# Which engine squares and adds the pairs of x behind the two mixer outputs

## What is computed

```
def rms_norm(x, g):
    y = xf * lax.rsqrt(jnp.mean(xf * xf, axis=-1, keepdims=True) + EPS)
for layer in range(DEPTH):          # DEPTH = 2: recurrent mixer, then attention mixer
    hn = rms_norm(x, norm_mix_g[layer])
    mix = rglru_mixer(hn, ...) if layer % 2 == 0 else dsa_mixer(hn, ...)
    x = x + mix
    x = x + sq_relu_mlp(rms_norm(x, norm_mlp_g[layer]), mlp_w_up[layer], mlp_w_down[layer])
```

## Time and profile before

| | us |
|---|---|
| median of 3 runs | 905.74 |
| lowest, highest | 905.62, 906.69 |
| time of the profiled execution | 907.54 |
| its span in the profile | 905.9 |
| PE busy in it | 874.5 |
| DVE busy | 688.9 |
| ACT busy | 469.6 |
| POOL busy | 161.1 |

### The profile page before, as it was taken

How to read it: one execution, slowest core, us unless ns; L and a number is a source line. 1 busy time by engine, 2 the same in 40 slices (tenths; PEclk the granted TensorE clock), 3 DMA queues, 4 the chain that set the end, 5 groups by cost and what they waited for, 6 DMA issues and landing times.

```text
span 905.9 us, 17923 instructions
## 1 busy us (share of the span) xinstructions
PE 874.5 (97%) x6992; PEld 831.8 (92%) x6992; DVE 688.9 (76%) x1066; ACT 469.6 (52%) x689; POOL 161.1 (18%) x172
## 2 busy tenths in 40 slices
PE   6999999999999987899999999999999999999998
PEld 5998899999999985599999999999899998999998
DVE  5796688889876697677666666668658998997793
ACT  7782355565444346735655444354357546645641
POOL 6221500013311000042000122232203223013000
PEclk9999999999999997999999999999999999999999
DMA  9754576678997431045655655565545544545542
GB/s 346 241 193 149 172 282 222 224 277 286 285 270 205 142 120 67 2 141 188 204 187 185 190 186 185 186 199 181 172 137 185 163 154 151 174 152 184 177 152 93
DMA packets 46961, 167.87 MB, mean 185 GB/s; under 512 B 5776, under 2 KB 5920, under 8 KB 46640
## 3 DMA queue, kind: packets, MB, share of 16 engines
q1 hardware_dynamic: 40896, 146.82, 48.6%
q0 software_dynamic: 5856, 20.00, 7.9%
q10 hardware_dynamic: 144, 0.15, 0.1%
HBM read 165.50 MB, written 1.44 MB: 184 GB/s over the span
## 4 chain that ended last, share of the span: by engine, by line
PE 72%; DVE 16%; ACT 5%; issue 5%; DMA 1%; DVEq 0%; POOL 0%; ACTq 0%; SPq 0%; POOLq 0%
PE bank L561 19%; PE bank L562 19%; PE bank L563 19%; DVE wlo L1321 5%; PE bank L628 5%; ACT whi L968 2%; DVE ada_prod L1472 2%; DVE ada_prod L1496 2%; PE bank L646 2%; PE bank L788 1%; DVE tq L1527 1%; PE bank L883 1%; PE bank L893 1%; PE bank L842 1%; PE bank L843 1%
## 5 line engine op out<-in xcount | busy, mean ns | idle before, releaser
L1321 DVE TENSOR_TENSOR wlo<-raw,whi 128x1024 fp32r<-128x1024 f32 x260 | 325.6, 1285 | 96.4 <-ACT whi L968 95.3
L561 PE MATMUL bank<-xh,whi 128*128 128x256 f32 x1328 | 375.4, 283 | 6.3 <-DVE vv L1906 1.5
L562 PE MATMUL bank<-xl,whi 128*128 128x256 f32 x1328 | 370.5, 279 | 0.0
L563 PE MATMUL bank<-xh,wlo 128*128 128x256 f32 x1328 | 370.1, 279 | 0.0
L968 ACT ACTIVATE whi<-raw 128x1024 fp32r<-128x1024 f32 x260 | 266.1, 1052 | 145.4 <-PE bank L563 121.4
L561 PEld LDWEIGHTS bank<-xh,whi 128*128 128x128 f32 x1328 | 249.3, 188 | 17.1 <-issue 10.2
L562 PEld LDWEIGHTS bank<-xl,whi 128*128 128x128 f32 x1328 | 249.2, 188 | 0.2
L563 PEld LDWEIGHTS bank<-xh,wlo 128*128 128x128 f32 x1328 | 249.0, 188 | 0.0
L561 PE MATMUL bank<-hhi,whi 128*128 128x256 f32 x512 | 143.3, 280 | 0.5 <-DVE wlo L1321 0.5
L562 PE MATMUL bank<-hlo,whi 128*128 128x256 f32 x512 | 143.1, 280 | 0.0
L563 PE MATMUL bank<-hhi,wlo 128*128 128x256 f32 x512 | 143.0, 279 | 0.0
(11 more groups left out here) (280 smaller groups left out, 1084.1 us busy)
## 6 DMA issues: line engine op xcount, KB each, us to landing
raw<-weights SPq DMA_DIRECT2D x260, 512.0 KB, 4.4
ada_raw<-ada_w POOLq DMA_DIRECT2D x24, 512.0 KB, 4.6
plain<-plain_w SPq DMA_DIRECT2D x16, 512.0 KB, 6.8
relB<-rel_scratch POOLq DMA_DIRECT2D x8, 256.0 KB, 7.2
bl<-rpb_in POOLq DMA_DIRECT2D x32, 64.0 KB, 3.6
x<-x_in SPq DMA_DIRECT2D x4, 256.0 KB, 6.1
cond<-cond_in POOLq DMA_DIRECT2D x1, 1024.0 KB, 7.3
cx<-ctx_in POOLq DMA_DIRECT2D x1, 1024.0 KB, 9.0
```

The costliest lines, as they stand in the source:

```text
L561: mmul(dst, hi, rh, start=start, stop=False)
L562: mmul(dst, hi, rlo, start=False, stop=False)
L563: return mmul(dst, lo, rh, start=False, stop=stop)
L1321: V_.tensor_tensor(wlo[:, sl], raw[:, sl], whi[:, sl].bitcast(F32), ALU.subtract)\
```

## The change

For the two seams, ACT squares each pair of x as one 128x512 instruction behind the two `xh`: the first pair goes straight into `acc`, the other three into `sqt`. DVE adds `sqt` to `acc` behind the two `xl`, for three of the four pairs. POOL has neither squares nor sums nor the zeroing of `acc` there; its four `ada` loads stand without them. The squares of the input at the start and those of the "down" stages stay on POOL. The counts of the two semaphores are moved accordingly.

```diff
-            def squares_by_pair(src, k, ready, after=None):
-                zero_acc(k)
+            def squares_of_input():
+                zero_acc(0)
                 for j in range(4):
-                    ready(j)
-                    add_squares(src[:, 2 * j:2 * j + 2], sqt[:], acc[:], j == 3)
-                    if after:
-                        after(j)
+                    pool.wait_ge(s_x[j], 16)
+                    add_squares(x[:, 2 * j:2 * j + 2], sqt[:], acc[:], j == 3)
...
-            squares_by_pair(x, 1, lambda j: pool.wait_ge(S_["x_lo_ready"], 8 + 2 * j + 2),
-                            after=lambda j: load_ada(2 + j))
+            for i in range(2, 6):
+                load_ada(i)
...
-            squares_by_pair(x, 4, lambda j: pool.wait_ge(S_["x_lo_ready"], 24 + 2 * j + 2))
...
+            def square_pair(i, j):
+                if j > 1:
+                    act.wait_ge(S_["tile_added"], ADD_PAIR[i] + j - 1)
+                A(sqt[:] if j else acc[:], x[:, 2 * j:2 * j + 2], ACT.Square).then_inc(S_["x_squared"], 1)
...
                 x_hi(2 * j, "g_mlp0")
                 x_hi(2 * j + 1, "g_mlp0")
+                square_pair(0, j)
...
                 x_hi(2 * j, "g_mlp1")
                 x_hi(2 * j + 1, "g_mlp1")
+                square_pair(1, j)
...
+            def add_pair(i, j):
+
+                if j:
+                    dve.wait_ge(S_["x_squared"], SQ_PAIR[i] + j + 1)
+                    if j > 1:
+                        dve.wait_ge(S_["tile_added"], ADD_PAIR[i] + j - 1)
+                    V_.tensor_tensor(acc[:], acc[:], sqt[:], ALU.add)\
+                        .then_inc(S_["tile_added" if j < 3 else "squares_summed"], 1)
...
                 x_lo(2 * j + 1, "g_mlp0", 8 + 2 * j + 2)
+                add_pair(0, j)
                 ada_tile(j)
...
                 x_lo(2 * j + 1, "g_mlp1", 24 + 2 * j + 2)
+                add_pair(1, j)
```

More of the change, by code:

```diff
@@ L317, in build @@
         L2_UNIT = U0["cg"] - 1
+        SQ_PAIR, SQ_DOWN = (0, 12), (4, 16)
+        ADD_PAIR, ADD_DOWN = (0, 9), (2, 11)
         @block.sync
@@ L421, in squares_by_tile @@
                         before(m)
-                    pool.wait_ge(S_["x_squared"], DT * i + m + 1)
+                    pool.wait_ge(S_["x_squared"], SQ_DOWN[i] + m + 1)
                     if m:
-                        pool.wait_ge(S_["tile_added"], (DT - 1) * i + m)
+                        pool.wait_ge(S_["tile_added"], ADD_DOWN[i] + m)
                     ins = G.tensor_tensor(acc[:, m % 2], acc[:, m % 2], sqt[:, 0], ALU.add)
@@ L428, in squares_by_tile @@
                         after(m)
-            squares_by_pair(x, 0, lambda j: pool.wait_ge(s_x[j], 16))
+            squares_of_input()
             pool.dma_start(cond[:], bass.AP(tensor=cond_in.tensor, offset=0, ap=[[0, P], [1, 2 * D]]))\
@@ L1103, in mlp @@
                     if m:
-                        act.wait_ge(S_["tile_added"], (DT - 1) * int(name) + m)
+                        act.wait_ge(S_["tile_added"], ADD_DOWN[int(name)] + m)
                     A(sqt[:, 0], x[:, m], ACT.Square).then_inc(S_["x_squared"], 1)
```

## The result

The changed kernel took 900.31 us (median of 16 runs, 895.47 to 904.56) against 905.98 of the kernel before on the same chip (16 runs): a ratio of 0.9934, 95% interval 0.9913 to 0.9956. The profiled execution took 896.13 us, 11.41 less than that of before; the prediction had found 3.72 us to win.

The account below looks back on a forecast made before the run. PE, busy 97% of the span, was taken to bound the kernel, so only its idle time could be won: 2.76 us (attention seam) + 0.96 (recurrent seam) = 3.72 us, from 905.74 to 902.0 us, range 901.2 to 904.0.

Parts of the forecast that it names:

- The cause: Attention seam: POOL's square and sum lengthen DVE's wlo pair to 4.04 us from 2.36, costing 1.68 us per pair.
- T: Start of an add to x in the attention seam; adds predicted at 388.37, 394.03, 399.7 and 405.44 us.
- The attention seam: From attention output into up1: DVE's cycle falls to 5.42 us, three PE holes close, gain 2.76 us.
- a hole is the distance of two starts less 0.12: Attention seam: counting rule giving PE holes of 0.79, 1.64 and 0.33 us, together 2.76 us.
- The recurrent seam: Behind the recurrent output: PE's wait behind up0's first unit goes, gain 0.96 us, between 0 and 0.96.
- rival (b): Recurrent seam: its gain is given back to the DMA pile-up, 903.0 us; chance 0.06.
- it may land until 116.8 ... so I cost the move at nothing: up0: first raw load, behind the earlier context load, has 10.2 us to land; loss 0, bounds 0 to 0.96 us.
- Nothing behind the seams is tied to a fixed time: From up1 on: PE, DVE or loads they release set all timing, so the seams' gain reaches the end in full.
- (a): First Square of each seam brings a table load of 1.28 us: 902.4 us, or 903.8 by the page's price; chance 0.07.
- (c): Attention seam's gain is given back by another cover or a late seventh tile; 0.96 alone left, 904.8 us; chance 0.06.
- (d): Attention seam: wlo stays long without POOL, cycle becomes 7.09 us, 0.3 slower, 906.0 us; chance 0.05.
- (e): The change does not take POOL off the path, 905.7 us; chance 0.01.

Follow-up runs that it names:

- echo: The changed kernel, with POOL also doing its old squares and sums of the attention seam on spare tiles nobody reads; ratio 1.0010 to the kernel before.
- after: The changed kernel itself, in the 16 runs of the result, against the kernel before; 900.31 us, ratio 0.9934.
- again_b: The changed kernel run once more without any edit, 12 runs; ratio 0.9954 to the kernel before.
- cx_late: The changed kernel with the 1 MB context load sent behind the eighth ada load instead of ahead of up0's raw loads; median 899.62 us, ratio 0.9930 to before.
- none: The changed kernel without the pairs' eight Squares on ACT and six sums on DVE in both seams; median 897.72 us, ratio 0.9910 to before.
- again: The changed kernel run once more without any edit, 6 runs; ratio 0.9916 to the kernel before.
- att_only: The kernel before with only the attention seam changed; POOL still squares and adds behind the recurrent output; ratio 0.9936 to before.
- split: The changed kernel with up1's 15 units behind the square sum written out as 6 and 9, without a loop or added wait; ratio 0.9961 to before.
- hole: The changed kernel, with PE waiting ahead of up1's square sum for the next unit's second weight chunk; ratio 0.9969 to before.
- midhole: The changed kernel with up1 written out as in split, plus a PE wait ahead of up1's eighth unit; ratio 0.9980 to before.
- hole0: The changed kernel, with up1's first unit starting only when all eight tiles of xl are there; ratio 0.9996 to before.

## Why the prediction was wrong, and where it was right

- **The cause was right.** wlo 2.36, adds 5.65 apart, the last at T + 16.96 us (predicted 17.07), no table load, no hole; echo brings the 4.04 back by POOL's arithmetic alone.
- **The attention seam** was worth 3.05 us, not 2.76. The step that was mis-sized is "a hole is the distance of two starts less 0.12". Behind a hole the next distance is longer too. In the kernel before it is 0.19 instead of 0.12 us behind the first hole (406.03 to 406.22), 0.22 behind the second (409.87 to 410.09), and 0.32 instead of 0.21 between the first two matmuls of the square sum (413.88 to 414.20). Together that is the 0.3. The upper groups differ by 2.8 to 3.1 us (906.29, and 903.15 to 903.48 in after and again_b).
- **The recurrent seam** was worth 0.96 us at the square sum and nothing in the time: rival (b) came, which had 0.06. The step that failed is "it may land until 116.8 ... so I cost the move at nothing". That looked at when PE wants the chunk. But ACT and DVE write whi and wlo in front of emptying the second bank, so ACT wants it at 112.65, and the raw chunk came 1.5 us later (114.15). DVE then lags in up0, and PE pays in small waits for wlo (in after 0.32 at 143.99, 0.29 at 167.35, 0.33 at 178.83; before only 0.30 at 167.71). cx_late shows it: with the load moved there is no wait, and down0 starts 1.15 us earlier behind the last add than in the kernel before. The profile of none shows a second part: without the squares down0 starts 0.4 to 0.8 us earlier, so the 0.5 to 0.6 us that they put ahead of the three whi and wlo was not free either.
- **The step that failed most, and put the time below the range,** is a term that the sum had at nothing, PE's own time behind the seams: "Nothing behind the seams is tied to a fixed time: from up1 on, all is released by PE, DVE or loads that they release, so what is won at a seam moves to the end". It took 0.118 us per matmul as PE's own pace. There are two paces, and a seam without holes is followed by the shorter in half of its runs (30 of 58 over after, again, again_b, att_only and split) where the kernel before has 13 of 104. Times 6.7 to 6.9 us, that is 2.7 us more in the mean. Without it the change would stand at 906.29 - 3.1 = 903.2 against a forecast of 3.7 less: inside the range. That the change came out this much faster is luck as far as the prediction goes: nothing in its working pointed at it.
- **Rivals.** (a) fell: no load at the Square. (c) fell for the attention seam. (d) is the cycle that echo made, 7.0 to 7.1 us: 5 us slower than the change and 1.9 above before (upper groups), where its price said 0.3 above; 0.96 of the difference is the recurrent gain that it had counted. (e) fell.

**What stays open.** Why PE draws the one pitch or the other at a restart. The first two matmuls behind a square sum start 305 to 309 ns apart (59 such places in 15 profiles; one more has 195). At 306 or more the pitch behind was 117.8 in all 35 cases, at 305 it was 113.3 in 16 and 117.8 in 8. That is a sign and no cause. Nor is it known why 113.3 is more frequent behind a square sum of up1 that is reached without a wait: hole shows that the wait decides there, not how. It is no general rule. At the sum at 291 us PE never waits, and the pitch behind it is 117.8 in all 15 profiles; at up0's sum it is 113.3 in 8 of 13 profiles without a wait, and in 1 of 2 with one, the kernel before.

## What to carry to other kernels

Take VectorE's two-input operations and GpSimd's arithmetic apart in time before you count instructions: here moving the work onto busier engines won, since GpSimd's part cost DVE 1.68 us per pair. When a moved instruction frees a queue, look at who first wants the transfers that now start earlier or later; it is the engine that converts the data, not the one that uses it. And where a time has two groups, count matmuls in equal stretches of a full-clock run, and compare the groups and their shares, not medians.

## What was not expected of the hardware

- Matmuls of 128x256 at a granted clock of 1.00 start 117.8 or 113.3 ns apart, and one of the two can hold for 171 us (410.46 to 581.25 us in after). It costs 6.7 us in 1488.
- It changed only at breaks in the stream. A wait of 0.06 us turned it in midhole's profile, and with a wait of 0.32 us in front of the square sum 20 of 21 runs were in the upper group.
- An idle time of 2.34 us was followed by 0.50 of the clock for 3.3 us (hole0), while one of 1.48 us left it at 1.00. So a hole of 2.3 us cost 4.1.
